# Moving every on-chip buffer of a fused two-block kernel to multiples of 1024 bytes

## The reference

```
h = rmsnorm(x, norm_g);  proj = h @ w_in                    # 2048 -> 14336
ya = (bg * conv(cg * v) * silu(za)) @ w_out_a
yb = gelu(s5_scan(u)); yb = yb * sigmoid(yb @ w_glu + b_glu)
x  = x + (sigmoid(ga) * ya + sigmoid(gb) * ((yb * silu(zb)) @ w_out_b)) @ w_o
u  = rms_norm(rmsnorm(x, final_g), norm1_g_2);  proj = u @ w_in_2      # q, k, v and RWKV inputs
h  = x + concat(dilated_attention(q, k, v), rwkv7(z)) @ w_out_2
h  = h + (silu(gate) * up) @ w_down_2                       # 5632 hidden
```

## Time and profile before

| | |
|---|---|
| median of 3 runs | 2275.11 us (2267.45 to 2280.07) |
| the profiled execution, its own time | 2278.84 us |
| its span, first to last instruction | 2277.1 us |
| TensorE busy | 2218.3 us |
| TensorE weight loads busy | 2164.1 us |
| VectorE busy | 1570.3 us |
| ScalarE busy | 1035.5 us |
| GpSimd busy | 264.2 us |
| HBM read | 384.29 MB |

### The profile page before, as it was taken

One profiled execution on the slowest core, in us unless ns is written; L12 is line 12 of the kernel. 1 busy time (PEld: TensorE's weight loads), 2 busy tenths in 40 slices (PEclk: granted clock), 3 DMA queues, 4 the chain that ended last, 5 costly groups with the idle time before them and its releaser, 6 DMA issues.

```text
span 2277.1 us, 51586 instructions
## 1 busy us (share of the span) xinstructions
PE 2218.3 (97%) x20554; PEld 2164.1 (95%) x20554; DVE 1570.3 (69%) x2072; ACT 1035.5 (45%) x1341; POOL 264.2 (12%) x176
## 2 busy tenths in 40 slices
PE   7999999999999999999999999799999999999997
PEld 6999999999999989999999788699999999999997
DVE  6889998889545667768766677576666666654444
ACT  5544444444544445566344344554433334433442
POOL 0344444444100000100011000000000000000000
PEclk9999999999999999999999899999999999999999
DMA  7555555555555556555655011255555555556553
GB/s 249 172 170 183 177 177 178 178 185 187 185 187 189 185 197 193 183 174 176 203 176 181 30 49 58 66 185 185 186 185 187 187 184 185 185 171 190 185 181 131
DMA packets 106960, 387.81 MB, mean 170 GB/s; under 512 B 12016, under 2 KB 12144, under 8 KB 106608
## 3 DMA queue, kind: packets, MB, share of 16 engines
q1 hardware_dynamic: 104544, 377.36, 51.0%
q0 software_dynamic: 1888, 7.87, 1.0%
q10 hardware_dynamic: 432, 1.21, 0.1%
HBM read 384.29 MB, written 2.10 MB: 170 GB/s over the span
## 4 chain that ended last, share of the span: by engine, by line
PE 92%; DVE 5%; ACT 2%; issue 1%; DMA 1%; DVEq 0%; ACTq 0%
PE ps_main L1672 28%; PE ps_main L1674 27%; PE ps_main L1673 27%; PE ps_aux L1900 2%; DVE w_lo L968 2%; PE ps_main L1900 1%; PE ps_main L1971 1%; ACT w_hi L493 1%; PE ps_aux L1921 1%; PE ps_main L1973 0%; PE ps_main L1972 0%; PE ps_aux L1741 0%; PE ps_aux L1729 0%; DMA w_raw<-wmain 0%; PE ps_aux L1818 0%
## 5 line engine op out<-in xcount | busy, mean ns | idle before, releaser
L968 DVE TENSOR_TENSOR w_lo<-w_raw,w_hi 128x1024 fp32r<-128x1024 f32 x718 | 918.8, 1296 | 470.1 <-ACT w_hi L493 464.9
L493 ACT ACTIVATE w_hi<-w_raw 128x1024 fp32r<-128x1024 f32 x718 | 748.9, 1047 | 751.4 <-PE ps_main L1674 735.9
L1672 PE MATMUL ps_main<-xs,w_hi 128*128 128x256 f32 x1664 | 467.8, 281 | 2.7 <-DVE w_lo L968 1.8
L1673 PE MATMUL ps_main<-xs,w_hi 128*128 128x256 f32 x1664 | 464.5, 279 | 0.0
L1674 PE MATMUL ps_main<-xs,w_lo 128*128 128x256 f32 x1664 | 464.3, 279 | 0.0
L1672 PE MATMUL ps_main<-x3s,w_hi 128*128 128x256 f32 x1408 | 394.4, 280 | 0.0
L1674 PE MATMUL ps_main<-x3s,w_lo 128*128 128x256 f32 x1408 | 392.8, 279 | 0.0
L1673 PE MATMUL ps_main<-x3s,w_hi 128*128 128x256 f32 x1408 | 392.8, 279 | 0.0
L1672 PEld LDWEIGHTS ps_main<-xs,w_hi 128*128 128x128 f32 x1664 | 312.4, 188 | 9.5 <-DVE w_lo L968 5.4
L1674 PEld LDWEIGHTS ps_main<-xs,w_lo 128*128 128x128 f32 x1664 | 312.6, 188 | 0.0
L1673 PEld LDWEIGHTS ps_main<-xs,w_hi 128*128 128x128 f32 x1664 | 311.4, 187 | 0.0
(11 more groups left out here) (413 smaller groups left out, 3770.6 us busy)
## 6 DMA issues: line engine op xcount, KB each, us to landing
w_raw<-wmain SPq DMA_DIRECT2D x622, 512.0 KB, 3.4
w_raw<-wdown SPq DMA_DIRECT2D x80, 512.0 KB, 3.7
w_raw<-wdown SPq DMA_DIRECT2D x16, 256.0 KB, 2.7
bias<-bias POOLq DMA_DIRECT2D x8, 384.0 KB, 3.3
x_res<-xt POOLq DMA_DIRECT2D x4, 512.0 KB, 6.7
out<-x_res SPq DMA_DIRECT2D x4, 512.0 KB, 2.6
x_first<-xt SPq DMA_DIRECT2D x2, 512.0 KB, 5.9
x_first<-xt ACTq DMA_DIRECT2D x2, 512.0 KB, 9.4
```

The lines of the kernel that those rows point to most:

```text
L493: nc.scalar.activation(whi[:, s, 0:width], raw[:, s, 0:width], ACT.Copy).then_inc(hi_ready, 1)
L968: V.tensor_tensor(wlo[:, s, 0:width], raw[:, s, 0:width], whi[:, s, 0:width].bitcast(F32), ALU.subtract)\
L1672: nc.tensor.matmul(out, whi[:, s, w], high[:, k, :], start=(first and kk == 0), stop=False)
L1673: nc.tensor.matmul(out, whi[:, s, w], low[:, k, :], start=False, stop=False)
```

## The change

No instruction, loop, wait or size changes. Only the places of the buffers in each partition do. The diff:

```diff
-        base = -(-nc.sbuf_base // 64) * 64
+        base = -(-nc.sbuf_base // 1024) * 1024
...
-        const = at("const", 66 * K, [NCONST])
-        small = 73 * K
+        const = at("const", 64 * K + 1344, [NCONST])
+        small = 72 * K
...
-        gg = at("gg", small + 14 * K, [KB])
-        phi = at("phi", small + 14 * K + 64, [STATE_TILES])
-        rho = at("rho", small + 14 * K + 192, [STATE_TILES])
-        work = small + 14 * K + 320
+        work = small + 14 * K
+        gg = at("gg", work + 120 * K, [KB])
+        phi = at("phi", work + 120 * K + 64, [STATE_TILES])
+        rho = at("rho", work + 120 * K + 192, [STATE_TILES])
```

## The result

The changed kernel takes 2311.89 us (median of 4 runs, 2310.32 to 2313.12) against 2274.95 us before (4 runs, 2267.45 to 2280.07). The ratio is 1.0161, with a 95% interval of 1.0139 to 1.0183: 1.6% slower, 37 us. The forecast was slower too, 2332 us against 2275, 57 us.

A forecast was written before the change was run, and what follows sets the result against it. The prediction took TensorE's matmul pace as the bound. To the profiled 2278.8 us it added 56 us for alignment and nothing for other parts, giving 2335, or 2332 us against the median (+2.5%); 8-in-10 range 2195 to 2365 us.

The forecast's parts named there:

- What bounds the kernel.: Whole kernel: TensorE's pace over its 17,040 stream matmuls sets the time; TensorE is busy 2218.3 of 2277.1 us.
- The whole kernel takes on the class of `x_raw_l`.: TensorE's stream: all moving blocks get distance 0 to the weights, as only `x_raw_l` in stage `u` had; 56 us slower.
- The term of 3.3 ns for 16,912 matmuls, 56 us.: TensorE's stream: each matmul not yet aligned like `x_raw_l` loses 3.3 ns, a price read in stage `u`; 56 us.
- The bounds of 85 and 169 us: TensorE's stream: half the matmuls clash at 10 ns, 85 us; or, as an outside case, all clash, 169 us.
- By 512.: TensorE's stream: the distance between moving and weight blocks counts by 512 bytes, going from 320 to 0 for all but `x_raw_l`.
- Splits, DMAs and tables at nothing.: ScalarE and VectorE splits, the stream's DMAs, and small tables and constants: their new addresses add nothing to the time.
- The rival of no change.: Whole kernel: addresses don't matter, 117.78 ns per matmul stays and the time is 2275 us; 14 in 100.
- The faster rival.: TensorE's stream: without crossings of multiples of 512 and 1024 it runs at 113.3 ns throughout, 2204 us; 28 in 100.

The follow-up runs named there:

- everything at 128: The changed kernel with the old base, so every buffer of the stream lies 128 above a multiple of 1024; 2313.79 us.
- 320: The changed kernel with `work` and so the moving blocks shifted up by 320 bytes, weights at 0 and 512; 2267.80 us.
- 448: The changed kernel with `work` and so the moving blocks shifted up by 448 bytes; 2238.71 us (median of 5 runs), ratio 0.9829 to the kernel before.
- distance 96: The changed kernel with `work` and so the moving blocks shifted up by 96 bytes; 2313.15 us.
- distance 64: The changed kernel with `work` and so the moving blocks shifted up by 64 bytes, weights at 0 and 512; 2278.43 us.
- distance 256: The changed kernel with `work` and so the moving blocks shifted up by 256 bytes, weights at 0 and 512; 2311.63 us.
- distance 192: The changed kernel with `work` and so the moving blocks shifted up by 192 bytes; 2233.73 us (median of 5 runs), ratio 0.9826 to the kernel before.
- 160: The changed kernel with `work` and so the moving blocks shifted up by 160 bytes; 2288.45 us.

## Why the prediction was right, and where it was off

*What bounds the kernel.* Right. Nearly the whole difference lies in TensorE's pace, the other engines' busy times are within 1 us, and `yos`, in which TensorE waits for units, did not grow.

*"The whole kernel takes on the class of `x_raw_l`."* Right in kind: the relation that only `x_raw_l` had became general, and it costs. The runs with everything at 128, with 320 and with 448 show that it is the relation of the two operands and not the place of either. That `x_raw_l` "has remainder 128 by 1024, like the weights" was the right thing to have noticed.

*The term of 3.3 ns for 16,912 matmuls, 56 us.* This is the mis-sized one. It measured 120.00 - 117.78 = 2.22 ns in the feed-forward stage, which by 16,912 is 37.5 us; the stretches that had been at 113.3, some 700 matmuls, lost 6.7 ns each, about 3 us more. The measured 37 us is a little less than this sum. Some 1 us of the rest is `yos`, which doesn't pass its loss on; what is left is small against the 13 us between the runs of the kernel before. The count that the prediction named as its direct test, 3,738 in 440 us before and 3,637 if the forecast held, came out at 3,669, between the two. What failed is reading a price for a uniform stream off a mixed one: a third of the matmuls at 120.0 and the others at 117.78 would average 118.5, and stage `u` was at 118.87. The stage `u` of distance 96 shows the same from the other side. There `x_raw_l` is at distance 0 and `x_raw_h` at 96, each a relation that gives 120.0 when all matmuls have it, and the mixture is at 24.9 / 70 / 3 = 118.6 ns, where the changed kernel has 24.8 / 69 / 3 = 119.8:

```profile
L1673 PE MATMUL ps_main<-x_raw_l,w_hi x71: 275/279/281, 41.1 to 66.0; 128*128 128x256 f32 x71
```

So the pace of a mixture is not the mean of its parts. The prediction named this as the thing it could least read, and that is where it went off. The bounds of 85 and 169 us were further off; they took a difference of durations (290 against 280 ns) for one of distances, and in the changed kernel the duration rose by 3 ns and the distance by 2.2.

*The range.* It went from 2195 to 2365 us and held all three cases, slower, no change and faster, so that the time lies in it says little. The forecast itself gave slower 58 in 100, on one operand of one stage. The narrower range of that case, 2300 to 2365, holds 2311.9 near its lower end.

*"By 512."* Wrong, without effect on the forecast, since 0 by 512 is also 0 by 256.

*Splits, DMAs and tables at nothing.* Right: 1,225 and 1,058 ns, 3.3 and 3.6 us, and the kernel of distance 64, which has all the rest of the change and the paces of the kernel before, took 2278.4 us in its one execution, within the spread of before.

*The rival of no change.* Fell: 2275 us was the sum by it, and the changed kernel takes 2311.9. The Trainium skill's rule that TensorE waits on no one ("SBUF — State Buffer", "Who interferes with whom") is about operations of different engines. On that, this case agrees with it: the pace is the same, 117.8 before and 120.0 after, whether VectorE, ScalarE and GpSimd run or not. That places don't matter, which the prediction took from it, does not follow. With one line of the layout edited, TensorE's pace in the feed-forward stage goes from 113.3 to 120.0 ns, so what is met lies among TensorE's own accesses. That it is its two read streams, moving blocks and weight blocks, that meet is the simplest reading, since their distance is what was varied; how they meet is not shown.

*The faster rival.* Fell for this change, since no crossing mattered: distance 256 crosses no multiple of 512 with a weight block and everything at 128 crosses all, and both are at 120.0. Its price was roughly sound, though. It said that 113.3 ns throughout would be 2204 us; distance 192 has it in some seven tenths of the stream, and takes 2234 us.

*What stays open.* What chooses between 117.78 and 113.3 after an interruption at distances 64, 192 and their like isn't settled; in the traces of distance 192, 320 and 64 a pace is kept from one interruption of the stream to the next. Nor is it settled why 160 and 96 differ. That the runs of the changed kernel lie within 3 us and those of before within 13 would fit a choice between two paces in the one and none in the other; only one execution of each was profiled, so this is argued. Outside stage `u`, setting the high and low halves at different distances wasn't tried, nor `w_hi` and `w_lo`.

## What to carry to other kernels

When TensorE is the bound and nobody is waited for, read its pace from start to start and compare stages; two paces for one shape are a lead. Round addresses are no goal in themselves: in this kernel equal remainders of moving and weight operands by 256 gave the slowest pace (120.0 ns, which only distance 96 had too), and one line that set the moving blocks 192 bytes past the weights' alignment was worth 3.4% against it (2233.73 to 2311.89 us). An effect seen on one operand in a mixed stream gave here the sign of what happens when all have it, and not its size.

## What the runs showed of the hardware

The pace of a stream of matmuls, each 128 by 128 stationary and 128 by 256 moving in 32-bit numbers with a weight load of its own, at full granted clock, by the distance of the two operands' starts in the partition, by 256 bytes:

| distance | feed-forward stage | other stages |
|---|---|---|
| 0 | 120.0 | 120.0 |
| 32 | 116.7 | 117.8 in the down projection and most of `xs` |
| 64 | 117.8 | 117.8; 113.3 in parts of the `rkv` columns and, in one run at 320, the whole down projection |
| 96 | 120.0 | 120.0 |
| 128 | 118.7 | 118.7; 120.0 in `wo` |
| 160 | 118.7 | 118.7 in the down projection; 117.4 in `gb`, `outa` and others |
| 192 | 113.3 | 113.3 in the down projection, `wo` and most of `xs`; 117.8 in `outa` and others |
| 224 | 118.3 | 118.3 |

Of each pair that should be alike on this ring, 0 and 256, 64 and 320, 192 and 448, both were run, and both members of a pair showed the same one or two paces. The best is not the farthest, and the ring is not symmetric. Whether VectorE, ScalarE, GpSimd or DMAs were active in a stretch made no difference at distances 0 and 320, in the feed-forward stage and the down projection. None of them reached the 106.7 ns of 256 columns at 2.4 GHz.
